# Expert weights loaded one whole matrix at a time, with three spare buffers used by every odd pair of experts

## What is computed (reference, cut)

```python
def hierarchical_moe(x2, w_rg, b_rg, w_re, b_re, w_gate, w_up, w_down):
    ...
    def run_block(args):
        tok, g, e = args
        xb = x2[tok]
        hb = jax.nn.silu(xb @ w_gate[e]) * (xb @ w_up[e])
        return (hb @ w_down[e]) * g[:, None].astype(x2.dtype)
```

## Time and profile before

| | |
|---|---|
| time, median of 3 executions | 1461.64 us (1461.43 to 1467.13) |
| profiled execution, its own time | 1467.38 us |
| its span | 1465.5 us |
| TensorE busy (matmul), share of the span | 1255.7 us, 86% |
| VectorE, ScalarE, GpSimd busy | 468.6, 263.6, 320.5 us |
| chain that ended last | TensorE 64%, DMA 24%, VectorE 6%, others 2% or less |
| experts' stage | from about 249 us to about 696 us |
| moved by DMA | 335.71 MB, mean 229 GB/s |

### The profile page before, as it was taken

How to read it: one execution, slowest core, us unless ns; L and a number is a source line. 1 busy time by engine, 2 the same in 40 slices (tenths; PEclk the granted TensorE clock), 3 DMA queues, 4 the chain that set the end, 5 groups by cost and what they waited for, 6 DMA issues and landing times.

```text
span 1465.5 us, 18473 instructions
## 1 busy us (share of the span) xinstructions
PE 1255.7 (86%) x7497; PEld 807.5 (55%) x7497; DVE 468.6 (32%) x1174; ACT 263.6 (18%) x683; POOL 320.5 (22%) x336
## 2 busy tenths in 40 slices
PE   8999999766576756666998789999999899999997
PEld 6864544322222312221776549999447664999843
DVE  4342624101100100010204624444573213544457
ACT  4313521000000000000224622111002322211100
POOL 5000100000000000000001433878200103587800
PEclk9999999987878877788998999999999999999999
DMA  9632234999999999999926008654344009654400
GB/s 328 227 109 93 115 124 160 421 421 421 422 422 422 422 422 422 422 422 414 340 78 230 1 24 264 201 174 173 110 149 144 1 33 298 200 189 170 147 1 29
DMA packets 112917, 335.71 MB, mean 229 GB/s; under 512 B 6648, under 2 KB 58160, under 8 KB 88269
## 3 DMA queue, kind: packets, MB, share of 16 engines
q1 hardware_dynamic: 110230, 326.33, 58.4%
q0 software_dynamic: 2416, 8.30, 1.6%
q10 hardware_dynamic: 199, 0.06, 0.0%
HBM read 333.59 MB, written 2.86 MB: 230 GB/s over the span
## 4 chain that ended last, share of the span: by engine, by line
PE 64%; DMA 24%; DVE 6%; ACT 2%; POOL 2%; issue 2%; SPq 0%; DVEq 0%; POOLq 0%; ACTq 0%
DMA ring<-in_w_expert_up 23%; PE bank L816 21%; PE bank L1533 17%; PE bank L1583 8%; PE bank L1159 5%; PE bank L1687 2%; PE bank L1390 1%; PE bank L981 1%; PE bank L1453 1%; PE bank L1363 1%; DVE small L2619 1%; PE bank L822 1%; PE bank L811 1%; PE bank L1347 1%; ACT arena L1996 1%
## 5 line engine op out<-in xcount | busy, mean ns | idle before, releaser
L1159 PE MATMUL bank<-ring,arena 128*32 128x512 f32 x976 | 153.8, 775 | 115.4 <-DMA ring<-in_w_expert_up 113.0
L1159 PEld LDWEIGHTS bank<-ring,arena 128*32 128x32 f32 x976 | 42.0, 137 | 223.5 <-issue 223.5
L816 PE MATMUL bank<-wide_rows,ring 128*128 128x256 f32 (+3 forms) x672 | 151.6, 380 | 2.2 <-DVE arena L2187 1.7
L816 PEld LDWEIGHTS bank<-wide_rows,ring 128*128 128x128 f32 (+1 forms) x672 | 125.9, 194 | 26.4 <-issue 6.3
L1533 PE MATMUL bank<-R,arena 128*128 128x128 f32 x1056 | 125.1, 275 | 0.0
L1533 PEld LDWEIGHTS bank<-R,arena 128*128 128x128 f32 x1056 | 121.5, 192 | 0.0
L2452 DVE TENSOR_TENSOR arena<-arena,bank 64x512 f32<-64x512 f32 x16 | 11.1, 691 | 301.5 <-ACT arena L1890 301.5
L816 PE MATMUL bank<-ring,wide_rows 128*128 128x512 f32 (+2 forms) x256 | 102.6, 556 | 0.2 <-issue 0.2
L1533 PE MATMUL bank<-wide_rows,ring 128*128 128x128 f32 x704 | 91.3, 275 | 4.9 <-ACT wide_rows L1875 4.2
L2923 POOL MEMSET arena<- 128x768 f32 (+2 forms) x3 | 1.1, 412 | 431.0 <-DVE X L2547 431.0
L1533 PEld LDWEIGHTS bank<-wide_rows,ring 128*128 128x128 f32 x704 | 84.8, 192 | 5.8 <-ACT wide_rows L1875 4.7
(11 more groups left out here) (383 smaller groups left out, 1815.0 us busy)
## 6 DMA issues: line engine op xcount, KB each, us to landing
ring<-in_w_expert_down SPq DMA_DIRECT2D x32, 2048.0 KB, 23.8
ring<-in_w_expert_up SPq DMA_DIRECT2D x31, 2048.0 KB, 23.7
ring<-in_w_expert_gate SPq DMA_DIRECT2D x30, 2048.0 KB, 19.2
ring<-in_ffn_w_in SPq DMA_DIRECT2D x44, 1024.0 KB, 7.8
ring<-in_ffn_w_out SPq DMA_DIRECT2D x10, 2048.0 KB, 8.1
ring<-in_w_in SPq DMA_DIRECT2D x7, 2048.0 KB, 15.9
ring<-in_shared_w_kv SPq DMA_DIRECT2D x3, 2048.0 KB, 7.8
ring<-in_w_out SPq DMA_DIRECT2D x2, 2048.0 KB, 8.7
```

The lines of the kernel that those rows point to most:

```text
L816: last = pe.matmul(dst, lhsT, rhs, start=k == 0, stop=k == len(pairs) - 1)
L1159: last = pe.matmul(bank[e % 2][at:at + SLOTS, :], xg_tile(e % 2, k)[:, SLOTS * r:SLOTS * r + SLOTS], w[r][:, kk, :], start=k == 0, stop=k ...
```

## The change

A unit becomes one whole matrix of one expert: 16 KB in a row for each lane in place of 2 x 8 KB. The six units of a pair are gate a, gate b, up a, up b, down a, down b. Pair by pair the six kinds keep fixed places: in even pairs all six are in the ring, in odd pairs the three first are in the spares and the three last in the ring. So there are nine buffers throughout. To make the second spare one piece, `arena` and `mem_kv` become one tensor; the first spare moves up to end with `rowvec`.

`moe_gate_up` waits for all four matrices at half 0, and `moe_down` for both of its own, since every half now reads a half of each. A slot is free when both halves are through: the waits of SP go to `pairs * 2`. The down matrices of the last pair are loaded as four halves, the lower halves first. The load of `g_final` waits for the last pair, whose gate is in the spare that covers `rowvec`. The second block's units come to other slots of the ring; their order stays.

```diff
-DUO_UNITS = ("gate", "up", "gate", "up", "down", "down")
+DUO_UNITS = ("gate", "gate", "up", "up", "down", "down")
...
-        mem_kv = sb("mem_kv", [P, 4, 2, MEM])
+        arena_and_mem = sb("arena", [P, ARENA + UNIT // 2])
+        arena = arena_and_mem[:, 0:ARENA]
+        mem_kv = arena_and_mem[:, ARENA:].rearrange("p (a b c) -> p a b c", b=2, c=MEM)
...
-        spare = [[wide_rows[:, 0:half_unit], rowvec[:, :, :].rearrange("p a d -> p (a d)")],
-                 [mem_kv[:, :, :, :].rearrange("p a b c -> p (a b c)"), arena[:, ARENA - half_unit:ARENA]],
-                 [arena[:, r * half_unit:(r + 1) * half_unit] for r in range(2)]]
+        at_xt = KT * S1 - half_unit
+        spare = [wide_rows[:, at_xt:at_xt + UNIT], arena_and_mem[:, ARENA - half_unit:ARENA + half_unit], arena[:, 0:UNIT]]
...
-                elif what[:-1] in ("gate", "up"):
-                    sp.wait_ge(moe["gate_up"], 2 * c + int(what[-1]) + 1)
-                elif what[:-1] == "down":
-                    sp.wait_ge(moe["down"], 2 * c + int(what[-1]) + 1)
+                elif what == "moe":
+                    sp.wait_ge(moe["down" if c >= 4 else "gate_up"], 2 * (DUOS - 1 if c < SPARES else DUOS))
...
-            def used_up(count, u):
-                sp.wait_ge(moe["down" if u >= 4 else "gate_up"], count + (u // 2 if u < 4 else u - 4) + 1)
+            def expert(u, pair, part=slice(0, UNIT)):
+
+                one = 2 * pair + u % 2
+                return experts[DUO_UNITS[u]][0].rearrange("e (p k) n -> p e (k n)", p=P)[:, one if isinstance(one, int) else bass.ds(one, 1), part]
+
+            def next_unit(u, pair, spared):
+
+                dst, arrived = (spare[u], spare_in[u]) if spared else (ring[:, (base + u) % RING, :], landed[(base + u) % RING])
+                src = expert(u, pair)
+                sp.dma_start(dst if isinstance(pair, int) else dst.rearrange("p (e m) -> p e m", e=1), src).then_inc(arrived, 16)
+
+            def used_up(u, pairs):
+                sp.wait_ge(moe["down" if u >= 4 else "gate_up"], pairs * 2)
...
             for u in range(SPARES, 6):
-                used_up(0, u - SPARES)
-                next_half(1, u, slice(2, 4))
-            for u in range(6):
-                used_up(0 if u < SPARES else 2, u + 6 - SPARES if u < SPARES else u)
-                next_half(2, u, slice(4, 6))
-            with sp.Fori(3, DUOS) as i:
+                used_up(u, 1)
+                next_unit(u, 1, False)
+
+            def odd_pair(i, parts=6):
+                for u in range(parts):
+                    used_up(u, i * 2 + (0 if u < SPARES else 1))
+                    next_unit(u, i * 2 + 1, u < SPARES)
+
+            def even_pair(i):
                 for u in range(6):
-                    used_up(i * 2 - 2, u)
-                    next_half(2, u, bass.ds(i * 2, 2))
+                    used_up(u, i * 2 + (1 if u < SPARES else 2))
+                    next_unit(u, i * 2 + 2, False)
+
+            even_pair(0)
+            with sp.Fori(1, DUOS // 2 - 1) as i:
+                odd_pair(i)
+                even_pair(i)
+            odd_pair(DUOS // 2 - 1, 4)
+            for half in range(2):
+                part = slice(half * half_unit, (half + 1) * half_unit)
+                for u in (4, 5):
+                    used_up(u, DUOS - 1)
+                    n = base + u
+                    sp.dma_start(ring[:, n % RING, part], expert(u, DUOS - 1, part)).then_inc(last_halves_in if half else landed[n % RING], 16)
...
             def moe_gate_up(e, half, i, first=False):
-                gate_w, up_w = arrived(e, 2 * half, i), arrived(e, 2 * half + 1, i)
+                gate_w, up_w = [[weights(e, u + r, half) for r in range(2)] for u in (0, 2)]
                 if half == 0:
+                    for u in range(4):
+                        arrived(e, u, i)
...
                 for half in range(2):
-                    w = arrived(e, 4 + half, i)
                     if half == 0:
+                        for u in (4, 5):
+                            arrived(e, u, i)
                         pe.wait_ge(moe["turned_copied"], i * 2 + (e + 1))
-                    outputs(e, half, w).then_inc(moe["down"], 1)
+                    elif e == DUOS - 1:
+                        pe.wait_ge(last_halves_in, 32)
+                    outputs(e, half, [weights(e, 4 + r, half) for r in range(2)]).then_inc(moe["down"], 1)
...
-            dve.wait_ge(rowvec_in, 16)
             empty_last("xTa", (cols[:, PACK["g_final"][0]:PACK["g_final"][0] + KT], None))
+            dve.wait_ge(rowvec_in, 16)
...
-            pool.wait_ge(moe["gate_up"], 3)
+            pool.wait_ge(moe["down"], 2 * DUOS)
             load_rowvec(g_final)
```

More of the change, by code:

```diff
@@ L107, in ring_units @@
     first = {"moe": len(order)}
-    order += [(f"{w}{u // 2 % 2 if u < 4 else u % 2}", e) for e in range(DUOS) for u, w in enumerate(DUO_UNITS) if e != 1 or u >= SPARES]
+    order += [("moe", u) for u in range(len(DUO_UNITS))]
     first["second"] = len(order)
@@ L502, in arrivals @@
                 return 0
+            if units[n][0] == "moe":
+                return 16 * (DUOS // 2 if units[n][1] < SPARES else DUOS)
             return 32 if units[n][0][:-1] == "ffn_in" else 16
@@ L697, in load @@
                     dst = slot(n, src.shape[1], src.shape[2])
-                elif what[:-1] in experts:
-                    dst, src = expert_half(what[:-1], int(what[-1]), n, slice(2 * c, 2 * c + 2))
+                elif what == "moe":
+                    dst, src = ring[:, n % RING, :], expert(c, 0)
                 else:
@@ L747, in _, with spare_half @@
             base = first_unit["moe"]
-            def spare_half(u, r):
-                _, src = expert_half(DUO_UNITS[u], u // 2, base, slice(2, 4))
-                sp.dma_start(spare[u][r], src[:, r, :]).then_inc(spare_in[u], 16)
-            spare_half(1, 0)
+            def spare_half(u, half):
+                part = slice(half * half_unit, (half + 1) * half_unit)
+                sp.dma_start(spare[u][:, part], expert(u, 1, part)).then_inc(spare_in[u], 16)
+            spare_half(1, 1)
             for u in (0, 2, 3):
@@ L758, in _ @@
             load(base + 1)
-            spare_half(1, 1)
+            spare_half(1, 0)
             spare_half(0, 1)
@@ L778, in _ @@
             with sp.If(more > 0):
-                last_pair = [duo_at(DUOS - 1, u) for u in range(6)]
-                for n in last_pair:
+                for n in range(base + SPARES, base + 6):
                     sp.wait_ge(landed[n % RING], use_count(n))
+                sp.wait_ge(last_halves_in, 32)
                 with sp.Fori(0, more) as p:
@@ L1188, in combine, with weights @@
                 return last
-            def by_expert(halves, u):
-                return [v.rearrange("p (k n) -> p k n", n=D if u >= 4 else HALF) for v in halves]
-            def weights_of(e, u):
-                slot = ring[:, duo_at(e, u) % RING, :]
-                return by_expert([slot[:, r * half_unit:(r + 1) * half_unit] for r in range(2)], u)
-            def arrived(e, u, i):
-                if e == 1 and u < SPARES and isinstance(i, int) and i == 0:
-                    pe.wait_ge(spare_in[u], 32)
-                    return by_expert(spare[u], u)
-                turn, e = (e - 2) // 2 if e > 2 else 0, e - 2 * ((e - 2) // 2) if e > 2 else e
-                n = duo_at(e, u)
-                pe.wait_ge(landed[n % RING], (i + turn) * 32 + use_count(n))
-                return weights_of(e, u)
+            def weights(e, u, half):
+                buffer = spare[u] if e % 2 and u < SPARES else ring[:, (base + u) % RING, :]
+                return buffer[:, half * half_unit:(half + 1) * half_unit].rearrange("p (k n) -> p k n", n=D if u >= 4 else HALF)
+            def arrived(e, u, i):
+                if e == DUOS - 1:
+                    e, i = 1, DUOS // 2 - 1
+                if e % 2 and u < SPARES:
+                    pe.wait_ge(spare_in[u], i * 16 + 32)
+                    return
+                loads = e + 1 if u >= SPARES else e // 2 + 1
+                pe.wait_ge(landed[(base + u) % RING], i * (32 if u >= SPARES else 16) + (use_count(base + u - RING) + 16 * loads))
             def moe_gather(quad, i):
@@ L1273, in _ @@
                             pe.wait_ge(ov["loaded"], p * (96 * DUOS) + i * 192 + 96 * (r + 1))
-                            gate_up(r, 0, weights_of(0, 0), weights_of(0, 1))
-                            gate_up(r, 1, weights_of(0, 2), weights_of(0, 3)).then_inc(ov["up"], 1)
+                            of_pair = lambda u, half: [weights(0, u + one, half) for one in range(2)]
+                            gate_up(r, 0, of_pair(0, 0), of_pair(2, 0))
+                            gate_up(r, 1, of_pair(0, 1), of_pair(2, 1)).then_inc(ov["up"], 1)
                             pe.wait_ge(ov["gated"], p * (DUOS // 2) + i + 1)
```

31 lines of the change are left out of this document (11 added, 20 removed).

## The result

| | before | after |
|---|---|---|
| median of 20 executions, the two kernels in turn on one chip | 1466.11 us (1461.04 to 1474.60) | 1473.91 us (1465.02 to 1477.56) |
| ratio, 95% interval | | 1.0042 (1.0027 to 1.0056) |
| profiled execution's span | 1465.5 us | 1472.0 us |

The ratio compares executions taken side by side. It is 6.2 us on 1466 us, between 4.0 and 8.2; the two medians by themselves differ by 7.8 us. The forecast was +1.4 us. The kernel is slower, by a little less than the 0.5% that the prediction called no change. The absolute time is 10.9 us above the forecast of 1463.0 and 2.9 us above the range's end of 1471. 4.5 of the 10.9 us come from the median before, which three executions had given as 1461.64.

The account below looks back on a forecast made before the run. The experts' stage was taken as bound by its weight loads on fully busy DMA engines. Start 5.5, gains' row -1.2, longer runs -6.5 and end 3.6 summed to +1.4 us: 1461.64 to 1463.0 us, range 1458 to 1471.

Parts of the forecast that it names:

- Longer runs: Experts' weight loads: 16 KB runs flow at 429 GB/s in place of 422, gaining 6.5 us (bounds 0 and 13.3).
- The start: First weight issues of the experts' stage: flow starts 3.5 us later, then pauses 2.0 us; costs 5.5 us.
- the gains' row: Load of `g_final`, 512 KB: leaves the experts' stage, gaining 1.2 us, and lands hidden with 5 us to spare.
- The end: Behind the last up landing: 64 matmuls wait instead of 32, the second 32 at high clock; costs 3.6 us.
- the bound of 6.9: Upper bound, in us, on the end's cost, if the added 32 matmuls run at the low clock throughout.
- TensorE's work there is untouched: Second block, behind the experts' stage: first units issued earlier, TensorE's work unchanged; no term in the sum.
- The middle: Pairs within the experts' stage: nine buffers gain nothing, coarser waits cost nothing, 3 us or more are left.

Follow-up runs that it names:

- e7: Kernel before, with only SP's first waits at the start changed to the new kernel's (both halves of pair 0); 1473.21 us, ratio 1.0046.
- e3: Changed kernel with 14, 5 and 3 matmuls on zeros ahead of the last pair's gate and up, transposes and down; 1469.99 us, ratio 1.0025.
- e4: Changed kernel with every unit after the first nine loaded as two 1 MB transfers with 8 KB runs; 1479.8 us, ratio 1.0091.
- e14: Repeat of e1, the changed kernel with one free gate unit issued ahead of two down units; 1465.82 us, ratio 0.9990.
- e11: Kernel before, unchanged, profiled again for a fourth trace; 1472.22 us in a single execution.
- e18: Kernel before with 3 matmuls on zeros (about 0.65 us) between the last combine and what follows; 1472.64 us, ratio 1.0049.
- e1: Changed kernel with gate a of pair 2, whose slot is free, issued ahead of pair 1's two down units; 1466.79 us, ratio 1.0004.
- the fill: Edit of e1 and e14 to the changed kernel: a free gate unit issued ahead of two down units; ratios 1.0004 and 0.9990.
- fill and zeros: Changed kernel with the fill, an early flag read and 6, 5 and 3 matmuls on zeros around the last pair's groups; 1466.84 us, ratio 1.0000.
- e2: Changed kernel with the last pair's two up units loaded as halves, lower halves first; 1469.18 us, ratio 1.0031.
- e6: Changed kernel with the fill, last up units as halves, early flag read, and 5 and 3 matmuls on zeros; 1469.4 us, ratio 1.0008.
- e16: Kernel before with the edits of both e7 and e9, late start and late end; 1476.37 us, ratio 1.0061.
- e9: Kernel before, with half 0 of the last pair's gate and up also waiting for half 1's units; 1474.96 us, ratio 1.0049.

## Why the prediction was off

The ratio gives +6.2 us where the sum had +1.4. The traces put the 4.5 us between +1.4 and their own +5.9 so: the end 2.1, the part behind the stage 3.8, the flow's part 0.3, and S -1.7.

- **Longer runs**, 6.5 us: right, 6.0 measured, and 428 GB/s.
- **The start**, 5.5 us: right, 5.4 measured (e7), late issue and pause as foretold. Together with the gains' row, which left the stage unseen, the flow's part came to -1.9 us; the sum had 5.5 - 1.2 - 6.5 = -2.2.
- **The end**, "The end costs 3.6 us", a sum of 5.34 + 3.64: the first step that failed, measured 5.7. It took the 64 matmuls of the changed kernel as one slow group and one fast one. TensorE now idles 6.6 to 6.9 us ahead of them, where it idled 1.3 to 3.2, and is at 1.2 GHz for about 5.4 us of them in the profiled execution. They took 9.73, 9.96 and 9.95 us where the sum had 8.98, and the group before took 5.34 three times and 3.64 once: +5.0. The down group, taken as 3.64 on both sides, is at the low clock for a part of it now more often: +0.7. In the mean the bound of 6.9 held. The mechanism, 64 matmuls behind the last landing and the first of them slow, was right, and e3 shows that the excess is the clock's: with TensorE kept busy they take 7.05 and 3.64 us. What decides when the clock rises stays open. It is not the length of the idle time: the same 64 took 8.68 us in e4 behind 6.4 us of it, and 9.36 us in e14 behind 7.5.
- **"TensorE's work there is untouched"**: the second step that failed. The work behind the stage is the same and takes 3.8 us more in the mean of the traces; where before and e11 differ, it is TensorE's time at a lower granted clock. The prediction priced it at nothing, though the kernel's own executions scattered by 6 us. e18 shows that a shift of 0.65 us at that place can cost 7 us with no more work than that, and the traces of e1 and e14 that the change with another start can have the short course again. Whether the change as such makes the long course more frequent, and why, stays open.
- **The middle**: right. The stretches read from 300 to 650 us have a share of 1.00 to 1.01, and a pair takes 646.08 - 616.73 = 29.35 us, against 29.83. The margin was smaller than written, though: the terms listed add up to 18.1 to 24.8 us, not 20.9 to 22.9, so that 1.5 us were left at worst, and not 3.
- **S** came 1.7 us earlier in the mean. It lies between 242.9 and 249.4 in all traces, with no order by kernel that could be found; it stays open.

The three-execution median of before was a poor zero as well: 4.5 us under that of 20.

No version beat the kernel before. The change with the fill (1.0004, 0.9990) and with fill and zeros (1.0000) cannot be told from it. In e14's trace the stage takes 444.9 us from S to C, against 445.7 in the mean before: the longer runs pay for the end, and little more.

## What to carry to other kernels

When a stage is bound by one stream of loads, add up what moves its start, its rate and the work behind its last landing, each by itself: here the start cost 5.4 us, the rate gave back 6.0, and the end cost 3 to 6. Coarser units pay at both ends of the stream, since the first slot comes free later and more work waits for the last one; another order of the first units brought the start's pause back here, and smaller first and last units are the next thing to try. And look at several executions of the kernel before as well: where TensorE works in short pieces, a shift of under a microsecond upstream changed the clock of a later stretch here, and that cost as much as the whole change.

## What the hardware showed that was not expected

- The DMA rate still rose from runs of 8 KB to 16 KB: 422 to 428 GB/s.
- Around a read of a flag and a branch TensorE was idle for 5.4 us (e2, e3); with the read elsewhere, for 4.4 us (e6). In the other traces a transfer landed later than that and hid it.
- After 6.6 to 6.9 us of idling 64 matmuls took 9.7 to 10.0 us, after 6.4 us (e4) 8.68, after 14.8 and 14.9 us (e16, e9) 9.33 and 8.99, right behind zeros (e3) 7.05. The longer wait did not cost more.
- The same 771 us of work took about 778 us in 7 of 20 traces. In the two traces of one kernel that were laid side by side (before, e11) the difference arises in one stretch of 102 us, on TensorE alone, at a granted clock of 0.87 in place of 0.93.
